# A two-layer block pair on one core: columns of a norm inside VectorE's operations, its bias added later by ScalarE

## The reference

```python
for l in range(DEPTH):
    h = x * (1.0 + scale[:, None, :]) + shift[:, None, :]
    y = ...            # even_mixer or mla_mixer
    x = layer_norm(DEEPNORM_ALPHA * x + (1.0 + gate[:, None, :]) * y, ln_g[l], ln_b[l])
...
def hybrid_layer(x, c_act, norm_g, w_ada, b_ada, w_in, w_out, pos):
    h = rms_norm_2(x, norm_g) * (1.0 + scale[:, None, :]) + shift[:, None, :]
    proj = h @ w_in
    ...
    return x + gate[:, None, :] * y
```

## Time and profile before

| | us |
|---|---|
| median of 3 runs | 1319.29 (1317.9 to 1320.32) |
| profiled execution | 1319.02 |
| its span | 1317.2 |
| TensorE busy | 1289.7 (98%) |
| VectorE busy | 941.3 (71%) |
| ScalarE busy | 580.2 (44%) |
| GpSimd busy | 357.4 (27%) |

### The profile page before, as it was taken

The page is one execution under the profiler, slowest core; times in us unless marked ns, Lnnn a source line. Parts: engine busy times, 40 slices in busy tenths (PEclk is TensorE's granted clock), DMA queues, the critical chain, the costliest instruction groups (busy, mean ns, idle before and its releaser), DMA issues.

```text
span 1317.2 us, 18039 instructions
## 1 busy us (share of the span) xinstructions
PE 1289.7 (98%) x6874; PEld 1106.0 (84%) x6874; DVE 941.3 (71%) x1415; ACT 580.2 (44%) x889; POOL 357.4 (27%) x262
## 2 busy tenths in 40 slices
PE   5999999999999999999999999999999999999997
PEld 5998888778898888888888878888888988888887
DVE  7765654796777558888678888776785577776663
ACT  1422322321264347666422587653452477734441
POOL 1200210055620004655434221122115322221122
PEclk9999999999999999999999999999999999999999
DMA  9565666537725620111234311213533111212111
GB/s 376 171 199 180 187 201 193 158 117 204 234 79 153 174 87 21 41 52 51 88 122 142 112 65 64 96 53 110 154 97 115 65 64 65 95 55 75 64 64 64
DMA packets 35093, 155.18 MB, mean 118 GB/s; under 512 B 6848, under 2 KB 9024, under 8 KB 23744
## 3 DMA queue, kind: packets, MB, share of 16 engines
q1 hardware_dynamic: 35008, 154.04, 36.9%
HBM read 151.92 MB, written 2.10 MB: 117 GB/s over the span
## 4 chain that ended last, share of the span: by engine, by line
PE 88%; DVE 5%; issue 3%; ACT 1%; POOL 1%; DMA 1%; SPq 0%; DVEq 0%; POOLq 0%; ACTq 0%
PE bank L971 25%; PE bank L973 24%; PE bank L972 24%; PE bank L1334 2%; PE bank L1319 1%; PE bank L1338 1%; PE bank L1179 1%; DVE keep L2477 1%; PE bank L1510 1%; PE bank L1537 1%; PE bank L1535 1%; DMA ada_first<-adat 1%; PE bank L1307 1%; PE bank L1306 1%; PE bank L978 1%
## 5 line engine op out<-in xcount | busy, mean ns | idle before, releaser
L971 PE MATMUL bank<-h_lo,w_hi 128*128 128x512 f32 (+1 forms) x1064 | 407.1, 383 | 0.7 <-DVE k_both L2045 0.5
L973 PE MATMUL bank<-h_hi,w_hi 128*128 128x512 f32 (+1 forms) x1064 | 402.5, 378 | 0.0
L972 PE MATMUL bank<-h_hi,w_lo 128*128 128x512 f32 (+1 forms) x1064 | 402.2, 378 | 0.0
L1883 DVE TENSOR_TENSOR w_lo<-w_raw,w_hi 128x2048 fp32r<-128x2048 f32 (+2 forms) x91 | 207.1, 2275 | 75.6 <-ACT w_hi L1557 75.4
L971 PEld LDWEIGHTS bank<-h_lo,w_hi 128*128 128x128 f32 x1064 | 200.2, 188 | 37.6 <-issue 1.8
L973 PEld LDWEIGHTS bank<-h_hi,w_hi 128*128 128x128 f32 x1064 | 200.1, 188 | 37.7
L972 PEld LDWEIGHTS bank<-h_hi,w_lo 128*128 128x128 f32 x1064 | 200.3, 188 | 36.3 <-issue 0.2
L1557 ACT ACTIVATE w_hi<-w_raw 128x2048 fp32r<-128x2048 f32 (+2 forms) x91 | 166.7, 1832 | 89.7 <-PE bank L973 72.9
L1925 DVE SCALAR_TENSOR_TENSOR acc<-ada_raw,cond_four,acc 128x1024 f32<-128x1024 f32 x62 | 87.5, 1411 | 3.9 <-DMA ada_raw<-adat 1.0
L1685 ACT ACTIVATE tmp<-bank 128x512 f32<-128x512 f32 x48 | 28.8, 600 | 112.3 <-PE bank L973 111.1
L2477 DVE TENSOR_TENSOR_SCAN keep<-keep,rmats 128x127 f32<-128x127 f32 (+2 forms) x64 | 57.8, 942 | 1.0
(11 more groups left out here) (359 smaller groups left out, 2688.1 us busy)
## 6 DMA issues: line engine op xcount, KB each, us to landing
w_raw<-wt SPq DMA_DIRECT2D x83, 1024.0 KB, 5.5
ada_raw<-adat SPq DMA_DIRECT2D x256, 128.0 KB, 2.9
ada_first<-adat SPq DMA_DIRECT2D x16, 512.0 KB, 12.2
ada_raw<-adat SPq DMA_DIRECT2D x32, 256.0 KB, 5.7
w_raw<-wt SPq DMA_DIRECT2D x8, 640.0 KB, 3.9
spare_raw<-wt SPq DMA_DIRECT2D x3, 1024.0 KB, 5.1
x<-xt SPq DMA_DIRECT2D x4, 512.0 KB, 15.5
out<-outf SPq DMA_DIRECT2D x16, 128.0 KB, 1.8
```

What stands on the lines that cost most here:

```text
L971: pe.matmul(dst, ah, bl, start=start, stop=False, skip_group_check=True)
L972: pe.matmul(dst, al, bh, start=False, stop=False, skip_group_check=True)
L973: return pe.matmul(dst, ah, bh, start=False, stop=stop, skip_group_check=True)
L1883: dve.tensor_tensor(w_lo[wb[T]][:, 0:n], w_raw[wb[T]][:, 0:n], f(w_hi[wb[T]][:, 0:n]), ALU.subtract).then_inc(w_lo_done, 1)
```

## The change

The norm's gain moves into VectorE's two operations: x = (x * g) * r, then x = (mean * r) * (-g) + x. A new column `gain_neg` holds -g. The bias is added inside the scaled norm, tmp = (x + b) * rho, and ScalarE adds it to `x` itself afterwards, when the scaled norm has read `x` (it waits on `h_t` instead of `ln_t`). The scaled norm no longer waits for ScalarE (`x_new`) but for VectorE's own plain norm of the block (`ln_t`). The lists of both engines are rewritten in part 2: VectorE does plain(j), scaled(j), low(j-1).

```diff
--- before.py
+++ after.py
@@ -436,6 +436,7 @@
         st_mr = place("st_mr", [P, NB], F32)
         gain_sq = place("gain_sq", [P, DC], F32)
         gain_bias = place("gain_bias", [P, DC], F32)
+        gain_neg = place("gain_neg", [P, DC], F32)
         gain_cols = place("gain_cols", [P, 3], F32)
         gain_part = place("gain_part", [P, 3], F32)
         gain_sum = place("gain_sum", [P, 3], F32)
@@ -1580,8 +1581,8 @@
             def affine(j):
 
                 k, tok = BLOCK[j]
-                act.wait_ge(ln_t, j + 1)
-                act.activation(x[:, k, tok], x[:, k, tok], ACT.Identity, scale=col("ln_g", DC + k),
+                act.wait_ge(h_t, H_T_BASE[2] + j + 1)
+                act.activation(x[:, k, tok], x[:, k, tok], ACT.Identity,
                                bias=col("ln_b", DC + k)).then_inc(x_new, 1)
 
             def blocks(l, part):
@@ -1589,22 +1590,12 @@
                 if part == 0:
                     act.wait_ge(cols_done, l)
                 if l == 2:
-                    if part == 0:
-                        affine(0)
-                        affine(1)
-                        high(2, 0)
-                        affine(2)
-                        high(2, 1)
-                        affine(3)
-                    elif part == 1:
-                        high(2, 2)
-                        high(2, 3)
-                    else:
-                        affine(4)
-                        for j in range(5, ITEMS):
-                            affine(j)
-                            high(2, j - 1)
-                        high(2, ITEMS - 1)
+                    for j in (range(0, 2), range(2, HALF_BLOCKS), range(HALF_BLOCKS, ITEMS))[part]:
+                        high(2, j)
+                        if j > 0:
+                            affine(j - 1)
+                    if part == 2:
+                        affine(ITEMS - 1)
                     return
                 for j in (range(0, 3), range(3, HALF_BLOCKS), range(HALF_BLOCKS, ITEMS))[part]:
                     high(l, j)
@@ -2090,11 +2081,19 @@
                 k, tok = BLOCK[j]
                 if j in (0, HALF_BLOCKS):
                     dve.wait_ge(stb_scale, 2 * l - 1 + (j > 0))
-                link(dve.tensor_tensor(x[:, k, tok], x[:, k, tok], bank[:, 6, tok], ALU.mult))
+                if l == 2:
+                    link(dve.scalar_tensor_tensor(x[:, k, tok], x[:, k, tok], col("ln_g", DC + k), bank[:, 6, tok],
+                                                  ALU.mult, ALU.mult))
+                else:
+                    link(dve.tensor_tensor(x[:, k, tok], x[:, k, tok], bank[:, 6, tok], ALU.mult))
                 if j in (0, HALF_BLOCKS):
                     dve.wait_ge(stb_done, si + 1)
+                if l == 2:
+                    dve.scalar_tensor_tensor(x[:, k, tok], bank[:, 5, tok], gain_neg[:, k:k + 1], x[:, k, tok],
+                                             ALU.mult, ALU.add).then_inc(ln_t, 1)
+                    return
                 dve.tensor_tensor(x[:, k, tok], x[:, k, tok], bank[:, 5, tok],
-                                  ALU.subtract).then_inc(h_t if l == 1 else ln_t, 1)
+                                  ALU.subtract).then_inc(h_t, 1)
 
             def scaled(l, j, si):
 
@@ -2102,9 +2101,11 @@
                 if j in (0, HALF_BLOCKS):
                     dve.wait_ge(stb_done, si + 1)
                 if l == 2:
-                    dve.wait_ge(x_new, DC + j + 1)
-                dve.tensor_tensor(tmp[:, j % 2, tok], x[:, k, tok], bank[:, 4 if l == 2 else 6, tok],
-                                  ALU.mult).then_inc(h_t, 1)
+                    dve.wait_ge(ln_t, j + 1)
+                    dve.scalar_tensor_tensor(tmp[:, j % 2, tok], x[:, k, tok], col("ln_b", DC + k), bank[:, 4, tok],
+                                             ALU.add, ALU.mult).then_inc(h_t, 1)
+                    return
+                dve.tensor_tensor(tmp[:, j % 2, tok], x[:, k, tok], bank[:, 6, tok], ALU.mult).then_inc(h_t, 1)
 
             def blocks(d):
 
@@ -2127,14 +2128,11 @@
                     low(2, 3)
                     derived_root(rho)
                     plain(2, 4, si)
-                    plain(2, 5, si)
                     scaled(2, 4, rho)
-                    for j in range(6, ITEMS):
+                    for j in range(5, ITEMS):
                         plain(2, j, si)
-                        low(2, j - 2)
-                        scaled(2, j - 1, rho)
-                    low(2, ITEMS - 2)
-                    scaled(2, ITEMS - 1, rho)
+                        scaled(2, j, rho)
+                        low(2, j - 1)
                     low(2, ITEMS - 1)
                     dve.memset(f(q_low[64:P, 0, :]), 0.0)
                     dve.memset(f(q_low[0:64, 1, :]), 0.0)
@@ -2410,6 +2408,7 @@
                     g, b = col("ln_g", DC, DC), col("ln_b", DC, DC)
                     link(dve.tensor_tensor(gain_sq[:], b, b, ALU.mult))
                     link(dve.tensor_reduce(gain_part[:, 2:3], gain_sq[:], AX.X, ALU.add))
+                    dve.tensor_scalar(gain_neg[:], g, -1.0, None, ALU.mult)
                     dve.tensor_tensor(gain_sq[:], g, g, ALU.mult)
                     link(dve.tensor_tensor(gain_bias[:], g, b, ALU.mult))
                     dve.tensor_copy(gain_cols[:, 0:1], ones[:, 0:1])
```

## The result

| | before | after |
|---|---|---|
| median (12 runs each, same chip) | 1319.02 us | 1320.96 us |
| lowest to highest | 1317.9 to 1320.32 | 1319.81 to 1323.29 |
| profiled execution | 1319.02 | 1320.73 |
| its span | 1317.2 | 1318.9 |

The ratio of the medians' runs is 1.0017, with an interval of 1.0009 to 1.0025: slower by about 0.17%, 1.9 us. The forecast was 1320.9.

The account below looks back on a forecast made before the run. TensorE bounds the kernel, waiting at the border for VectorE's last `h_lo`. Left half +0.5 and right half +1.1 make +1.6 us, with ScalarE's adds hidden: 1320.9 us from a median of 1319.29, range 1318.3 to 1323.1.

Parts of the forecast that it names:

- What bounds the kernel: Border of layers two and three: TensorE, busy 1289.7 of 1317.2 us, waits for VectorE's last `h_lo`, later for `k_both`.
- Dearer operations: VectorE's norms: 36 `tensor_tensor` become `scalar_tensor_tensor` with a column as scalar, 0.06 us more each, three to a block.
- A wait inside the block: Right half: the scaled norm directly behind its block's plain norm waits for it, 0.11 us in each of eight blocks.
- Left half: Blocks 0 to 3: twelve dearer VectorE operations make the right half's statistics and broadcasts 0.5 us later, all passed on.
- Right half: From block 4's first plain operation to the start of the last `h_lo`, 17.6 us before: +1.1 us in sum.
- The one new wait: Ahead of the last `h_lo`: VectorE waits for GpSimd's `tmp` of block 11, slowed to 1.14 us beside `h_lo`; +0.8 us.
- TensorE's restart: Border's end: TensorE goes on near 767.6 after the wait for the last `h_lo`, instead of 766.04.
- ScalarE's adds: Behind the last `h_hi`: bias adds of blocks 10 and 11 at 0.72 us each; `w_hi` near 767.8, 2.7 us later.
- A cheaper last `h_lo` alone wins nothing, because this chain would still hold 1.6.: Behind the border: ScalarE's chain `av_both`, `w_hi`, scans, `k_both` is also 1.6 us later, matching TensorE's own path.
- VectorE pays for the neighbourhood: Rival, 0.12: right-half `h_lo` beside GpSimd lengthen, four narrow by 0.28 and three wide by 0.37 us; 1323.1 us.
- the waits are free: Rival, 0.14: waits inside a block cost VectorE nothing, taking 0.9 us off both chains; 1320.0 us.
- nothing costs: Rival, 0.06: neither scalar column nor wait costs anything; the right half gets about 1.0 us shorter; 1318.3 us.

Follow-up runs that it names:

- run 4: Changed kernel's order and waits, but plain tensor_tensor operations with gain and bias left out of VectorE's operations; 1318.78 us, ratio 0.9997 to the kernel before.
- run 1: Changed kernel, but the right half's scaled norm reads old buffer by_gain and needs no wait on the plain norm; 1320.31 us, ratio 1.0011 to the kernel before.
- run 5: Changed kernel with two more wide ScalarE operations behind its two adds at the border's end, ahead of w_hi; 1321.56 us, ratio 1.0022 to the kernel before.
- run 2: Changed kernel with right-half turns ordered plain(j), low(j-1), scaled(j); 1320.73 us, ratio 1.0015 to the kernel before.
- run 9: Changed kernel with a PSUM-reading 128x256 tensor_tensor between scaled norm and h_lo in seven right-half turns; 1323.05 us, ratio 1.0028 to the kernel before.
- run 7: Kernel before the change with one swap at the border's end: scaled(11) ahead of low(10); 1318.19 us, ratio 0.9996 to the kernel before.
- run 11: The same kernel as run 7 measured once more; 1318.31 us, ratio 0.9993 to the kernel before.
- run 8: As run 7, and the low part of block 2 moved behind the right half's first statistics on VectorE; 1318.31 us, ratio 0.9992 to the kernel before.

## Why the prediction was right, point by point

- **What bounds the kernel.** Right. TensorE's last wait for `h_lo` and the wait for `k_both` stayed where they were, and the 1.7 us of the span lie in the border's stretch (1.69).
- **Dearer operations.** Forecast 0.06 us each; measured 0.20 us in a wide turn of three (run 4), 0.067 each. All 36 together cost 1.93 us in the stretch, 0.56 in the left half and 1.36 in the right one; my sum had 0.5 and 1.4.
- **A wait inside the block.** Forecast 0.11 us, eight times; measured 0.12 to 0.13 at each of the seven that run 1 can show (0.89 us together). The eighth, block 4's, lies under the wait for the broadcast, which I had at 0.2 us and which measured 0.24. The Trainium skill, page "VectorE: DVE Perf Modes", section "The DRAIN you can't avoid", has a semaphore between consecutive VectorE operations at no extra cost. Run 1 disagrees, by 0.12 to 0.13 us at each.
- **Left half.** Forecast +0.5; measured 0.52 and, undone alone, 0.50. ScalarE's two adds ahead of the root cost nothing: its idle time before the root is 0.22 us now, from 1.02.
- **Right half.** Forecast +1.1; measured +1.21. The one new wait, forecast at 0.8, is 0.75, and the last `h_lo` starts 2.10 us after the last scaled norm, forecast 2.07. One small term was too large: -0.3 for gaps ahead of four narrow `h_lo`. The trace of before has such a gap at two of them (750.10 to 750.52 and 751.64 to 752.04, instead of 0.33), about 0.16; the other two follow a wide operation without one. That is about the 0.11 by which the sum fell short.
- **TensorE's restart.** Forecast 767.6, measured 767.90. Of the 0.3, 0.13 are the later start of the border in this trace, where the clock was low just ahead of it, 0.11 the right half and 0.02 the left.
- **ScalarE's adds.** This term was mis-sized, by the step "I price an add by that turn too". An add takes a turn of 0.61 us, not 0.72 (run 5). `w_hi` came at 767.79 as forecast because the last `h_hi` came at 765.84 and not 765.65: two errors of opposite sign.
- **"A cheaper last `h_lo` alone wins nothing, because this chain would still hold 1.6."** Wrong. ScalarE had 0.41 us of idle time left before `av_both`, not none, and in run 2 the chain itself moved, since the last `h_hi` came earlier too: `w_hi` by 0.29 us, counted from the first plain operation. The other 0.38 came out of that idle time, and all 0.67 us by which the last `h_lo` came earlier arrived.
- **"VectorE pays for the neighbourhood."** It did not happen: every `h_lo` beside GpSimd in the right half kept 0.42 or 0.69 us. But the reason that I gave for it, that VectorE is first by 0.17 us, fell in run 9, where GpSimd was first by 0.15 and paid all the same. The forecast was right here for a reason that does not hold. The Trainium skill, page "SBUF — State Buffer", section "Who interferes with whom", says that the later to issue blocks; by the starts that the profile shows the turns of after agree in sign, run 9's 1.31 us does not, and runs 7 and 11 differ from each other at the same distance of 0.12 us.
- **The rivals' times.** That the waits are free (1320.0) is excluded by run 1, that nothing costs (1318.3) by run 4.

The chain to ScalarE that the change shortens was indeed not what anybody waited for. The two waits of 0.97 us went because no scaled norm stands behind the waiting `h_lo` of an earlier block any more. That needs nothing of the change but one line of VectorE's list: run 7 has it in the kernel before, for 0.93 us of the stretch and none of the costs. Of the kernels here it is the best, together with that of run 8 (stretches of 54.12 to 54.15, times of 1318.19 and 1318.31 us), by a margin that one measurement of it alone does not tell from none.

## What to carry to other kernels

Price a hop that you remove by who waits for its end: here nobody did, and 36 operations on the engine that is waited for became dearer by 0.06 us each. On an engine that runs back to back, do not put an operation directly behind the one that it depends on if other work can stand between: 0.12 to 0.13 us each time here. And look at the tail of a staggered list for a producer that stands behind an earlier block's waiting consumer; there nothing is left to fill the wait, and the two waits add up (two of 0.97 us here).

## What the runs showed of the hardware

- A per-partition column as the scalar in VectorE's operation cost 0.06 to 0.07 us at both widths (0.41 to 0.475 and 0.68 to 0.747), so it does not grow with the width here.
- A GpSimd operation of 0.77 us took 1.15 beside a wide `h_lo`, and 1.31 in run 9, where it started 0.15 us before that `h_lo` and beside one more operation: starting first did not spare it.
- Who pays is not fixed by the order of starts. With a wide `h_lo` 0.12 us behind the second of two GpSimd operations, that `h_lo` took 1.18 us instead of 0.69 in runs 7 and 8, and in run 11, the same kernel as run 7, GpSimd's pair took 2.04 us instead of 1.53.
- In single executions TensorE's granted clock fell to 0.50 (1.2 GHz) for some us in which TensorE was busy almost without a pause (3.91 to 4.00 of 4 us), from 732 to 740 us in four of the 13 traces; where that fell into the border it moved everything behind it, and it goes along with the scatter of 2 us and more between runs of one kernel.
